# Five different start addresses for the five slots of a weight ring

## What is computed

```python
z = h @ w_in                       # (512 x 1024) @ (1024 x 2048), 3072 or 9232 columns
... mixers: Fourier, neighbourhood attention, gated conv, retention, gated delta rule ...
h = h + y @ w_out                  # (512 x 1024) @ (1024 x 1024)
kv = m @ wkv; h = h + attend(h @ wq, kv) @ wo
h = h + (gelu(conv(h @ w_up)) * u) @ w_down   # twice with 2048, once with 2816 hidden features
```

## Time and profile before

| | |
|---|---|
| time, median of 2 runs | 2425.95 us (2424.82 to 2427.09) |
| time of the profiled execution | 2427.01 us |
| span from its first to its last instruction | 2425.2 us |
| PE busy | 2341.8 us, 97% of the span, 10934 matmuls |
| chain that ended last | PE 92%, DVE 5%, the rest 3% |
| POOL busy | 975.5 us, 40% |
| ACT busy | 858.1 us, 35% |
| mean share of the 16 DMA engines | 28.1% for the weight queue |
| mean granted TensorE clock | 0.990 of full speed |

### The profile page before, as it was taken

One profiled execution on the slowest core, in us unless ns is written; L12 is line 12 of the kernel. 1 busy time (PEld: TensorE's weight loads), 2 busy tenths in 40 slices (PEclk: granted clock), 3 DMA queues, 4 the chain that ended last, 5 costly groups with the idle time before them and its releaser, 6 DMA issues.

```text
span 2425.2 us, 25642 instructions
## 1 busy us (share of the span) xinstructions
PE 2341.8 (97%) x10934; PEld 1928.1 (80%) x10934; DVE 986.0 (41%) x1199; ACT 858.1 (35%) x1043; POOL 975.5 (40%) x394
## 2 busy tenths in 40 slices
PE   9989999999999999999999999988998999999998
PEld 7768878888887887888887668867877888888886
DVE  4241224441144122444137231577368333566611
ACT  4345333332322433433353452351452243322221
POOL 4317334444444733444435224320240144465641
PEclk9999999999999999999999999999999999999999
DMA  6215223333332422333333213320220023333322
GB/s 222 87 44 164 71 69 96 96 96 96 96 96 93 161 76 65 95 100 96 109 122 95 61 52 104 114 61 18 61 78 18 27 96 130 96 96 96 97 100 73
DMA packets 142769, 219.81 MB, mean 91 GB/s; under 512 B 11568, under 2 KB 68272, under 8 KB 142400
## 3 DMA queue, kind: packets, MB, share of 16 engines
q1 hardware_dynamic: 141104, 213.42, 28.1%
q10 hardware_dynamic: 1552, 4.76, 0.6%
HBM read 213.92 MB, written 4.23 MB: 90 GB/s over the span
## 4 chain that ended last, share of the span: by engine, by line
PE 92%; DVE 5%; ACT 1%; issue 1%; DMA 0%; POOL 0%; ACTq 0%; DVEq 0%
PE ps L999 76%; PE ps L1180 2%; PE ps L1183 2%; PE ps L1401 1%; PE ps L1196 1%; PE ps L1219 1%; DVE MT L2019 1%; PE ps L1390 1%; PE ps L1289 1%; PE ps L1302 1%; PE ps L1342 1%; DVE MM L2023 0%; PE ps L1474 0%; PE ps L1058 0%; PE ps L1418 0%
## 5 line engine op out<-in xcount | busy, mean ns | idle before, releaser
L525 POOL TENSOR_TENSOR w_lo<-w_raw,w_hi 128x1024 fp32r<-128x1024 f32 x378 | 967.6, 2571 | 1408.1 <-ACT w_hi L570 1407.7
L570 ACT ACTIVATE w_hi<-w_raw 128x1024 fp32r<-128x1024 f32 x378 | 394.2, 1055 | 876.1 <-DMA w_raw<-ffn_w_up 123.4
L999 PE MATMUL ps<-XH,w_hi 128*128 128x512 f32 x1784 | 698.8, 392 | 0.9 <-ACT RLN L821 0.9
L999 PE MATMUL ps<-XH,w_lo 128*128 128x512 f32 x1784 | 694.2, 389 | 0.0
L999 PE MATMUL ps<-XL,w_hi 128*128 128x512 f32 x1784 | 694.0, 389 | 0.0
L999 PE MATMUL ps<-HID,w_hi 128*128 128x512 f32 x1728 | 536.8, 392 | 8.1 <-DVE HID L1660 5.6
L999 PEld LDWEIGHTS ps<-XH,w_hi 128*128 128x128 f32 x1784 | 334.9, 188 | 73.0 <-issue 2.4
L999 PEld LDWEIGHTS ps<-XL,w_hi 128*128 128x128 f32 x1784 | 334.9, 188 | 71.5 <-issue 2.4
L999 PEld LDWEIGHTS ps<-XH,w_lo 128*128 128x128 f32 x1784 | 334.8, 188 | 69.9
L999 PEld LDWEIGHTS ps<-HID,w_hi 128*128 128x128 f32 x1728 | 326.2, 189 | 78.1 <-issue 6.8
L999 PE MATMUL ps<-HID,w_lo 128*128 128x512 f32 x864 | 337.8, 391 | 0.0
(11 more groups left out here) (350 smaller groups left out, 2354.2 us busy)
## 6 DMA issues: line engine op xcount, KB each, us to landing
w_raw<-w_in SPq DMA_DIRECT2D x72, 512.0 KB, 3.7
w_raw<-ffn_w_up SPq DMA_DIRECT2D x128, 256.0 KB, 2.9
w_raw<-w_up SPq DMA_DIRECT2D x88, 256.0 KB, 3.1
w_raw<-xa_wkv SPq DMA_DIRECT2D x32, 512.0 KB, 3.7
w_raw<-ffn_w_down SPq DMA_DIRECT2D x32, 512.0 KB, 3.7
w_raw<-w_in_c SPq DMA_DIRECT2D x24, 512.0 KB, 3.8
w_raw<-w_down SPq DMA_DIRECT2D x22, 512.0 KB, 3.7
w_raw<-xa_wq SPq DMA_DIRECT2D x16, 512.0 KB, 3.8
```

What stands on the lines that cost most here:

```text
L525: nc.gpsimd.tensor_tensor(w_lo[:, s, :, :], w_raw[:, s, :, :], w_hi[:, s, :, :].bitcast(F32), ALU.subtract).then_inc(lo_done, 1)
L570: nc.scalar.activation(w_hi[:, s, :, :], w_raw[:, s, :, :], ACT.Copy).then_inc(hi_done, 1)
L999: mm = nc.tensor.matmul(ps[:, bank + m, :], a, b, start=start and j == 0 and n == 0, stop=stop and j == 1 and n == 2)
```

## The change

The rings w_raw/w_lo and w_hi, each of five slots side by side, become one ring. Slot i holds the 4 KB of w_raw (and w_lo in the same place) and right behind them the 4 KB of w_hi, and it begins 8 KB times i plus SLOT_AT[i] bytes behind the ring's start. The ring's start and the arena keep their residue of 128 modulo 512, so the weights of slot 0 lie 4 bytes past the residue of XH, XL and the arena, those of slot 1 16 bytes, of slot 2 24, of slot 3 160 and of slot 4 176. Every address in a slot that an instruction names moves with it. The arena keeps its address; the small tables between ring and arena move up by 192 bytes.

No instruction is added, removed or moved on any engine, and no wait changes. In the changed kernel all weight operands go by the names of the ring tiles.

```diff
+SLOT_AT = (4, 16, 24, 160, 176)
...
-        w_raw = sb("w_raw", [P, RING, 2, UC])
-        w_lo = nc.alloc_sbuf_tensor_at("w_lo", [P, RING, 2, UC], F32R, offset=nc.sbuf_base - RING * 2 * UC * 4)
-        w_hi_at = nc.sbuf_base
-        w_hi = sb("w_hi", [P, RING, 2, UC], F32R)
+        ring_at = nc.sbuf_base
+        ring = sb("ring", [P, RING * 4 * UC + SLOT_AT[-1] // 4])
+        ring_r = nc.alloc_sbuf_tensor_at("ring_r", [P, RING * 4 * UC + SLOT_AT[-1] // 4], F32R, offset=ring_at)
+        w_raw, w_lo, w_hi = [], [], []
+        for i in range(RING):
+            c = i * 4 * UC + SLOT_AT[i] // 4
+            by_row = lambda flat, c: flat[:, c:c + 2 * UC].rearrange("p (j n) -> p j n", j=2)
+            w_raw.append(by_row(ring, c))
+            w_lo.append(by_row(ring_r, c))
+            w_hi.append(by_row(ring_r, c + 2 * UC))
...
-        a0 = nc.sbuf_base + (w_hi_at - nc.sbuf_base) % 512
+        a0 = nc.sbuf_base + (ring_at - nc.sbuf_base) % 512
...
-                nc.scalar.activation(w_hi[:, s, :, :], w_raw[:, s, :, :], ACT.Copy).then_inc(hi_done, 1)
+                nc.scalar.activation(w_hi[s][:, :, :], w_raw[s][:, :, :], ACT.Copy).then_inc(hi_done, 1)
...
-                            wt = w_lo[:, slot, j, :] if n == 2 else w_hi[:, slot, j, :]
+                            wt = w_lo[slot][:, j, :] if n == 2 else w_hi[slot][:, j, :]
```

More of the change, by code:

```diff
@@ L446, in load @@
                 for c, width in c_of:
-                    sp.dma_start(w_raw[:, slot, :, at_col:at_col + width],
+                    sp.dma_start(w_raw[slot][:, :, at_col:at_col + width],
                                  view[:, 2 * k:2 * k + 2, c:c + width]
@@ L453, in _ @@
             w0 = phases[0][1].rearrange("(k p) n -> p k n", p=P)
-            sp.dma_start(w_raw[:, 0, 0, :], w0[:, 0, 0:UC]).then_inc(w0_loaded, 16)
-            sp.dma_start(w_raw[:, 0, 1, :], w0[:, 1, 0:UC]).then_inc(w_loaded[0], 16)
+            sp.dma_start(w_raw[0][:, 0, :], w0[:, 0, 0:UC]).then_inc(w0_loaded, 16)
+            sp.dma_start(w_raw[0][:, 1, :], w0[:, 1, 0:UC]).then_inc(w_loaded[0], 16)
             for name, mat, nk, groups in phases:
@@ L466, in _ @@
                     view = mat.rearrange("(k p) n -> p k n", p=P)
-                    dst = w_raw[:, u % RING, :, :].rearrange("p a (b c) -> p (a b) c", c=P)
+                    dst = w_raw[u % RING][:, :, :].rearrange("p a (b c) -> p (a b) c", c=P)
                     at_col = 0
@@ L524, in lo @@
                 pool.wait_ge(hi_done, u)
-                nc.gpsimd.tensor_tensor(w_lo[:, s, :, :], w_raw[:, s, :, :], w_hi[:, s, :, :].bitcast(F32),
+                nc.gpsimd.tensor_tensor(w_lo[s][:, :, :], w_raw[s][:, :, :], w_hi[s][:, :, :].bitcast(F32),
                                         ALU.subtract).then_inc(lo_done, 1)
@@ L529, in _ @@
                 pool.wait_ge(w0_hi, j + 1)
-                nc.gpsimd.tensor_tensor(w_lo[:, 0, j, :], w_raw[:, 0, j, :], w_hi[:, 0, j, :].bitcast(F32),
+                nc.gpsimd.tensor_tensor(w_lo[0][:, j, :], w_raw[0][:, j, :], w_hi[0][:, j, :].bitcast(F32),
                                         ALU.subtract).then_inc(lo_done if j else w0_lo, 1)
@@ L634, in _ @@
                     act.wait_ge(w0_loaded, 16)
-                    nc.scalar.activation(w_hi[:, 0, 0, :], w_raw[:, 0, 0, :], ACT.Copy).then_inc(w0_hi, 1)
+                    nc.scalar.activation(w_hi[0][:, 0, :], w_raw[0][:, 0, :], ACT.Copy).then_inc(w0_hi, 1)
                 elif c == 1:
                     act.wait_ge(w_loaded[0], 16)
-                    nc.scalar.activation(w_hi[:, 0, 1, :], w_raw[:, 0, 1, :], ACT.Copy).then_inc(w0_hi, 1)
+                    nc.scalar.activation(w_hi[0][:, 1, :], w_raw[0][:, 1, :], ACT.Copy).then_inc(w0_hi, 1)
                 if c >= 2:
@@ L1056, in _ @@
                     for m in range(4):
-                        wt = (w_lo if n == 2 else w_hi)[:, 0, j, m * P:(m + 1) * P]
+                        wt = (w_lo if n == 2 else w_hi)[0][:, j, m * P:(m + 1) * P]
                         mm = nc.tensor.matmul(ps[:, m, :], wt, (XL if n == 1 else XH)[:, j, :], start=j == 0 and n == 0, stop=False)
@@ L1175, in kv @@
                                 for n in range(3):
-                                    wt = w_lo[:, s, j, :] if n == 2 else w_hi[:, s, j, :]
+                                    wt = w_lo[s][:, j, :] if n == 2 else w_hi[s][:, j, :]
                                     xt = ML[:, kt, :] if n == 1 else MH[:, kt, :]
@@ L1472, in ffn2 @@
                             for n in range(3):
-                                wt = (w_lo if n == 2 else w_hi)[:, s, j, m * P:(m + 1) * P]
+                                wt = (w_lo if n == 2 else w_hi)[s][:, j, m * P:(m + 1) * P]
                                 mm = nc.tensor.matmul(ps[:, m, :], wt, (hl if n == 1 else hh)[:, kt, :],
@@ L1507, in block2 @@
                 pe.wait_ge(rb_dve, 1)
-                hi = w_hi[:, u % RING, :, :].rearrange("p a (b c) -> p (a b) c", c=P)
-                lo = w_lo[:, u % RING, :, :].rearrange("p a (b c) -> p (a b) c", c=P)
+                hi = w_hi[u % RING][:, :, :].rearrange("p a (b c) -> p (a b) c", c=P)
+                lo = w_lo[u % RING][:, :, :].rearrange("p a (b c) -> p (a b) c", c=P)
                 for kt in range(KT):
```

## The result

The changed kernel takes 2470.3 us (median of 2 runs, 2468.62 to 2471.99) against 2425.95 us. The ratio of the runs is 1.018, 95% interval 1.016 to 1.021. The kernel is slower by some 44 us: that is clear of the noise, and the interval reaches over 2% on one side, so whether the loss is more or less than 2% stays undecided.

What follows compares the result with a forecast made beforehand. PE's back-to-back matmul stream was taken to bound the kernel. With the pace change and all small terms at 0, 2427.0 us stayed 2427, or 2426 against the median; the 8-in-10 range was 2345 to 2530.

Steps and rivals of the forecast that it cites:

- What bounds the kernel: PE's matmul stream, split matmuls of 512 columns following at 226.7 ns; 1983 of 2427 us use ring slots, all in series.
- The price of the new distance: Split matmuls using ring slots: change of pace when weights and streamed tile differ in residue; taken as 0, bounded 96 us less to 119 more.
- Rival 2: Matmuls of each slot: streams collide and the equal residue is good; 13.3 ns each, 24 us a slot; slower by over 2%: 0.29.
- Its second mechanism: Slots 0 and 2, at 4 and 24 bytes: a piece starting inside a group of 16 bytes takes one read more.
- Rival 1: Split matmuls: streams collide and the equal residue is bad; up to 19 us gained per clear slot; faster by over 2%: 0.21.
- the 10.7 ns over the plain matmuls: Fixed time each split matmul carries beyond a plain fp32 one; 96 us over 8928 matmuls if the layout causes it.
- The small terms: Beside PE: ACT's copies (1060 ns), POOL's subtractions (2400 ns), transfers (3.7 us) and moved addresses; each taken as 0.
- the forecast's own case of no effect: All ring-slot matmuls: the residue has no effect, time 2426 us, likeliest case 2420 to 2432; chance 0.32.
- the 0.18: Chance that the residue matters but the slots' effects together stay within 48 us: mixed signs, one or two slots, or few ns.
- the remaining 13.3 ns: Fixed part of each split matmul whatever its width, beside 213.3 ns for 512 columns; what an address could act on.

Runs made afterwards that it cites:

- the first map: The changed kernel with slots 0 to 4 at distances of 8, 32, 64, 128 and 256 bytes; 2459.22 us, one run.

## Why the prediction was right in its range and wrong in its reason

- **What bounds the kernel** held. PE's stream is the time: 42 us from the matmuls' pace against 41.6 in the span, so waits absorbed and added next to nothing.
- **The price of the new distance, taken as 0,** is the step that failed. It measured 4.95 ns on average, 42 us. The reason given for 0 was the plain fp32 pair of lines 1342 and 1219, equal at 592 ns at different residues. The text called that row weak because a plain stream reads at half the pace, and the runs bear this out: the plain matmuls of line 1203 stay at 6.91 us for 32 in every run, whatever the split ones do. A row of another form of the operation was no measure of this one. The uniform 389 ns of all split pairs, which looked like insensitivity, was one residue seen many times.
- **Rival 2**, the equal residue is a good one, is what happened, in the means of all five slots at once but at 3.5 to 6.9 ns for each and not at 13.3. Its price per slot, 24 us, is mis-sized by a factor of some 2 to 4: measured are 6 to 12 us (3.5 to 6.9 ns on some 1700 matmuls). Its second mechanism, a piece that starts inside a group of 16 bytes, isn't needed: 32 and 64 bytes lose as well, and so do most units at 16.
- **Rival 1**, that the 10.7 ns over the plain matmuls could be had by another layout, is refuted for 512 columns at the 25 distances tried; with 256 columns, 4% of the split matmuls, some distances are indeed faster (see the end). The Trainium skill's gap of N / 2.4 + 2.5 ns ("TensorE: Matmul & The Clock Gate", Back-to-back issue gap), by which the rival was weighed, is given there for a matmul by itself. It doesn't describe this stream: no run here shows a split matmul of 512 columns near 216 ns in its mean; 226.7 is the least. The other rule, two independent read ports and a PE that never waits on anyone ("SBUF — State Buffer", Who interferes with whom), speaks of ports and of other engines, not of addresses. What the prediction drew from it, that a residue can't matter, is contradicted: the same instructions take 226.7 or 233.3 ns with nothing changed but where the weights lie.
- **The small terms** at 0 held: POOL 2406 ns (2400), ACT 1060 (1060), transfers 3.7 us (3.7).
- **The range and the chances**: 2470 lies within 2345 to 2530, and 1.8% is within 2%, but the forecast's own case of no effect is out. The case that came, an effect of one sign in all slots that stays under 48 us, was counted among the 0.18. That the time lies so near to the forecast is luck: the range was wide for effects of both signs and larger size, and the same mechanism with 160 bytes in every slot is at 2.2%. That the kernel before already stood at the best distance for its stream, so that no slot could gain, was nowhere weighed.

What stays open is the mechanism. Shown are that moving the weights against the streamed tile is what changed the pace, that 256 bytes equal 0, that 160 bytes cost 16 cycles for each piece so placed, and that at distance 0 the 226.7 ns is lost with narrow loads and outputs. That the two reads meet somewhere in the chip is a guess that fits; no run shows it. Open are also why one distance can have two paces, and what the remaining 13.3 ns are.

## What to carry to other kernels

When a stream of fp32r matmuls bounds a kernel, put the tiles of both operands at the same residue modulo 256 bytes; it costs a few bytes of padding, and being off by as little as 4 bytes cost 2.5% of the stream's time here in one direction and 0.5% in the other. Read the pace from the distance between matmul starts, never from busy share, which was 97% in both kernels. And where every pair in a trace shares the property that a change removes, the trace says nothing about that property: a map with a different value in each ring slot measures five in one run. Read such a map unit by unit and not by means alone, since a mean can hide two paces, and confirm a value that matters with a run that has it in every slot.

## What the runs showed of the hardware that was not expected

- The pace of a split matmul depends on the distance between its weights and the streamed tile: 226.7 ns at 0 and 256 bytes, up to 234.2 ns at 96 with the activations streaming, unsmooth in between. With the weights streaming 0 and 256 stay good (226.7 and 227.3), and the others change: 229.1 at 64 bytes, 237.0 at 4.
- One distance can have two paces in one run: at 16 bytes units stood at 233.3 ns in the first block and at 226.8 in the last stretch.
- With 256 streamed columns the order is another: 192 matmuls took 22.64 us in the first map's run against 23.03 at distance 0. In that map the slot at 8 bytes has a mean of 115.6 ns, below the 119.9 of the equal residue.
- Loading 64 columns instead of 128, with half the output rows, made the 512-column stream slower at distance 0, 226.7 to 230.0 ns.
